# A two-layer hybrid encoder on one core: sums in their own banks, 192 keys, stepped pooling, and weight tiles prepared in quarters

## The reference

```
h = x @ w_in[l]                      # aq, ak, av, bq, bk, bv, cx
oa = local attention: 6 heads, chunks of 64 queries, each sees its own
     chunk of 64 keys and the one before, bias, softmax with a sink logit
ob = differential attention: 6 heads, two maps of 32 dims each,
     w = softmax(map 0) - lam * softmax(map 1), causal by chunks of 64
oc = pooling: means over windows of 2, 4, 8, 16 tokens less the input,
     a 64x64 matrix for each of 4 groups, times a scale
x = layer_norm(ALPHA * x + concat(oa, ob, oc) @ w_o[l])
u = conv3(x @ w_up[l]);  x = layer_norm(ALPHA * x + (silu(g) * u) @ w_down[l])
```

## Time and profile before

| what | value |
|---|---|
| median of 3 runs | 2726.92 us (2726.09 to 3502.72) |
| the profiled execution | 2722.3 us |
| its span | 2720.5 us |
| mean granted TensorE clock | 0.963 |
| instructions | 30437 |
| DMA | 249.03 MB, mean 92 GB/s |

### The profile page before, as it was taken

How to read it: one execution, slowest core, us unless ns; L and a number is a source line. 1 busy time by engine, 2 the same in 40 slices (tenths; PEclk the granted TensorE clock), 3 DMA queues, 4 the chain that set the end, 5 groups by cost and what they waited for, 6 DMA issues and landing times.

```text
span 2720.5 us, 30437 instructions
## 1 busy us (share of the span) xinstructions
PE 2491.2 (92%) x11608; PEld 2007.4 (74%) x11608; DVE 1503.7 (55%) x2845; ACT 831.3 (31%) x1709; POOL 1290.0 (47%) x724
## 2 busy tenths in 40 slices
PE   7987888999999999899998999988999989999996
PEld 5865666777777877777776877767777777788885
DVE  5256545566666385147666288056555555546436
ACT  1133314444442121035543122034444411222221
POOL 4532353434443655454444655543343445566662
PEclk7998999999999999999999999989999999999998
DMA  5633223332322323433322323432232122334331
GB/s 163 197 84 88 83 79 88 82 90 77 93 63 62 94 77 101 117 96 105 88 84 63 90 73 108 119 95 74 78 82 77 57 77 78 93 97 121 108 94 70
DMA packets 347264, 249.03 MB, mean 92 GB/s; under 512 B 37291, under 2 KB 306927, under 8 KB 347119
## 3 DMA queue, kind: packets, MB, share of 16 engines
q1 hardware_dynamic: 321792, 211.01, 26.2%
q10 hardware_dynamic: 25327, 36.07, 5.1%
HBM read 226.32 MB, written 20.71 MB: 91 GB/s over the span
## 4 chain that ended last, share of the span: by engine, by line
PE 65%; DVE 21%; ACT 5%; issue 4%; DMA 2%; POOL 1%; ACTq 1%; SPq 0%; DVEq 0%
PE psum L716 41%; PE psum L946 10%; PE psum L815 4%; PE psum L746 3%; PE psum L767 3%; DVE room L1209 3%; DVE room L1233 2%; DVE conv L1316 2%; PE psum L801 2%; ACT conv L1137 2%; DVE x_res L1520 2%; DVE conv L1338 2%; DMA w_raw<-in_w_in 1%; ACTq L981 1%; DVE x_res L1485 1%
## 5 line engine op out<-in xcount | busy, mean ns | idle before, releaser
L692 POOL CAST w_hi<-w_raw 128x1024 fp32r<-128x1024 f32 x360 | 405.2, 1125 | 1364.2 <-DMA w_raw<-in_w_up 699.7
L694 POOL TENSOR_TENSOR w_lo<-w_raw,w_hi 128x1024 fp32r<-128x1024 f32 x360 | 888.7, 2469 | 28.8
L716 PE MATMUL psum<-x_hi,w_hi 128*128 128x512 f32 x2048 | 848.5, 414 | 40.3 <-POOL w_lo L694 15.2
L716 PE MATMUL psum<-x_hi,w_lo 128*128 128x512 f32 x2048 | 814.4, 398 | 0.0
L716 PE MATMUL psum<-x_lo,w_hi 128*128 128x512 f32 x2048 | 813.2, 397 | 0.0
L716 PEld LDWEIGHTS psum<-x_hi,w_hi 128*128 128x128 f32 x2048 | 394.8, 193 | 139.1 <-issue 22.9
L946 PE MATMUL psum<-hid,w_hi 128*128 128x512 f32 x1408 | 451.2, 402 | 17.6 <-DVE x_res L1520 15.0
L716 PEld LDWEIGHTS psum<-x_hi,w_lo 128*128 128x128 f32 x2048 | 393.4, 192 | 87.8
L716 PEld LDWEIGHTS psum<-x_lo,w_hi 128*128 128x128 f32 x2048 | 395.8, 193 | 73.1 <-issue 1.7
L1316 DVE SCALAR_TENSOR_TENSOR conv<-psum,prm_all,conv 128x511 f32<-128x511 f32 x176 | 131.8, 749 | 490.1 <-ACT conv L1137 489.7
L946 PEld LDWEIGHTS psum<-hid,w_hi 128*128 128x128 f32 x1408 | 258.1, 191 | 79.1 <-DVE hid L1343 10.9
(11 more groups left out here) (126 smaller groups left out, 2339.0 us busy)
## 6 DMA issues: line engine op xcount, KB each, us to landing
w_raw<-in_w_up SPq DMA_DIRECT2D x176, 512.0 KB, 3.8
w_raw<-in_w_down SPq DMA_DIRECT2D x88, 512.0 KB, 3.6
w_raw<-in_w_in SPq DMA_DIRECT2D x36, 512.0 KB, 4.0
w_raw<-in_w_o SPq DMA_DIRECT2D x32, 512.0 KB, 4.1
qk_scratch<-stage_qk SPq DMA_DIRECT2D x48, 256.0 KB, 3.4
q_stack<-qk_scratch ACTq DMA_DIRECT2D x72, 128.0 KB, 2.9
k_stack<-qk_scratch ACTq DMA_DIRECT2D x36, 256.0 KB, 4.9
w_raw<-in_w_in SPq DMA_DIRECT2D x16, 384.0 KB, 3.4
```

The lines of the kernel that those rows point to most:

```text
L692: nc.gpsimd.tensor_copy(w_hi[:, slot, :], w_raw[:, slot, :]).then_inc(s["w_high"], 1)
L694: nc.gpsimd.tensor_tensor(w_lo[:, slot, :], w_raw[:, slot, :], w_hi[:, slot, :].bitcast(F32), ALU.subtract).then_inc(s["w_ready"], 1)
L716: mm = nc.tensor.matmul(o, w, v[:, k, :], start=(k == 0 and w is wh and v is x_hi[h]), stop=(k == KT - 1 and w is wl))
```

## The change

1. POOL cuts each tile in quarters of 256 columns: four casts without a wait between them, then four subtractions, each after its cast; the last one signals.
2. AV takes a dense bank of its own. `place_banks` gives each user of a dense bank (R, P and W of layer 0, V of layer 0, U, D, AV) the bank whose last user stands earliest in the list, and each bank has its own full and free semaphores. The waits for o_read are gone; the wait is for the bank.
3. Local heads leave out the 64 masked keys (`unseen`): scores, bias, exponential over 192 columns; the first of the two sums has 64 rows. The turning still takes both blocks whole.
4. Pooling is cut into events CW, two additions at a time, and `project` has a new order: c0, CW, bq0, CW, bk0, W0, c1, CW, bq1, CW, bk1, CW, bq2, W1, bk2, ak. `stages` is fitted to it; event PR now comes after two projected blocks instead of three.
5. V tiles of (0, 1) are no longer cut in parts and stand ahead of attention (0, 0), outside of the merge.
6. Shares: AV 0.6 to 0.9, AT 0.6 to 0.8, CW 1.0 each.

The core of the diff, without the many lines in which only a semaphore's name changes:

```diff
+    out = p("c0") + c((0, 0)) + p("bq0") + c((0, 1)) + p("bk0") + [("W", l, h, 0)] + p("c1") + c((1, 0))
+    out += p("bq1") + c((1, 1)) + p("bk1") + c((1, 2)) + p("bq2") + [("W", l, h, 1)] + p("bk2", "ak")
+    if (l, h) == (0, 1):
+        return values + out + p("aq0", "aq1", "aq2")
+    return out + values + [("AS", l, h)] + p("aq0", "aq1", "aq2")
...
-    return {"AV": 0.6, "AT": 0.6, "V": 0.5, "MR": 2.0, "LM": 2.0, "LE": 2.0, "LF": 1.5}.get(kind, 1.0)
+    return {"AV": 0.9, "AT": 0.8, "CW": 1.0, "V": 0.5, "MR": 2.0, "LM": 2.0, "LE": 2.0, "LF": 1.5}.get(kind, 1.0)
...
-    out = [("X", 0, i) for i in range(HT)] + first[:3] + [("PR",)] + first[3:4] + bias[:6] + first[4:5] + bias[6:]
-    out += [("N", 0)] + first[5:6] + [("N", 1)] + first[6:9] + [("N", 2)] + first[9:11] + [("N", 3)]
+    out = [("X", 0, i) for i in range(HT)] + first[:3] + [("PR",)] + first[3:5] + bias[:6] + first[5:7] + bias[6:]
+    out += [("N", 0)] + first[7:10] + [("N", 1)] + first[10:13] + [("N", 2)] + first[13:16] + [("N", 3)]
...
-    out += merge(left[:cut[0]], attend(0, 0))
+    out += left[:HT] + merge(left[HT:cut[0]], attend(0, 0))
...
+def unseen(h, u):
+
+    kind, head, t = unit_of(u)
+    return HD if kind == "a" and h * HT + t > 0 else 0
...
+def place_banks():
+
+    bank, read = {}, [-1] * 4
+    for e in EVENTS:
...
+        for key in keys:
...
+            n = min(range(4), key=lambda n: read[n])
+            assert read[n] < AT[e]
+            bank[key], read[n] = n, AT[last]
+    return bank
...
-                nc.gpsimd.tensor_copy(w_hi[:, slot, :], w_raw[:, slot, :]).then_inc(s["w_high"], 1)
-                pool.wait_ge(s["w_high"], n + 1)
-                nc.gpsimd.tensor_tensor(w_lo[:, slot, :], w_raw[:, slot, :], w_hi[:, slot, :].bitcast(F32),
-                                        ALU.subtract).then_inc(s["w_ready"], 1)
+                cuts = [slice(c, c + 256) for c in range(0, 1024, 256)]
+                for cut in cuts:
+                    nc.gpsimd.tensor_copy(w_hi[:, slot, cut], w_raw[:, slot, cut]).then_inc(s["w_high"], 1)
+                for q, cut in enumerate(cuts):
+                    pool.wait_ge(s["w_high"], 4 * n + q + 1)
+                    i = nc.gpsimd.tensor_tensor(w_lo[:, slot, cut], w_raw[:, slot, cut],
+                                                w_hi[:, slot, cut].bitcast(F32), ALU.subtract)
+                i.then_inc(s["w_ready"], 1)
...
-                for c in range(0, width, HALF):
+                for c in range(skip, width, HALF):
...
-                if u >= 1 and width_of(h, u)[1] > HALF:
-
-                    pe.wait_ge(s["o_read"], after(("AV", l, h, u - 1), "o_read"))
...
-                if u >= 1:
-                    pe.wait_ge(s["o_read"], after(("AV", l, h, u - 1), "o_read"))
+                take(e)
                 for b in range(width // P):
+                    seen = slice(unseen(h, u) if b == 0 else 0, P)
+                    mm = nc.tensor.matmul(ring_bank(e)[:, 0:HD], turned_w[h][seen, b * P:(b + 1) * P],
+                                          v_all[seen, lo + b, at:at + HD],
...
-                for dst in ((b1, b2) if c == 0 else (b1, b2, b1, b2)):
-                    at += w
-                    then(nc.vector.tensor_tensor(dst[:, at:], last[:, at:], last[:, at - w:HALF + PADC - w], ALU.add))
-                    last, w = dst, 2 * w
+                if step <= c:
+                    for last, dst, n in ((xs, b1, 0), (b1, b2, 1)) if step == 0 else ((b2, b1, 2), (b1, b2, 3)):
+                        w = 1 << n
+                        at = 2 * w - 1
+                        then(nc.vector.tensor_tensor(dst[:, at:], last[:, at:], last[:, at - w:HALF + PADC - w], ALU.add))
+                    return
```

More of the change, by code:

```diff
@@ L72, in project, with c @@
 def project(l, h):
[L73 to L77, removed]
     def p(*names):
[L80 to L86, removed]
+        out = []
+        for n in names:
+            if (l, h) == (0, 1):
+                out += [("Pp", l, h, n, part) for part in range(PARTS - 1)]
+            out.append(("P", l, h, n))
+        return out
+    values = [("V", l, h, i) for i in range(HT)]
+    def c(*steps):
+        return [("CW", l, h, *step) for step in steps]
+    out = p("c0") + c((0, 0)) + p("bq0") + c((0, 1)) + p("bk0") + [("W", l, h, 0)] + p("c1") + c((1, 0))
+    out += p("bq1") + c((1, 1)) + p("bk1") + c((1, 2)) + p("bq2") + [("W", l, h, 1)] + p("bk2", "ak")
+    if (l, h) == (0, 1):
+        return values + out + p("aq0", "aq1", "aq2")
+    return out + values + [("AS", l, h)] + p("aq0", "aq1", "aq2")
 def attend(l, h):
@@ L253, in signals @@
         if what[:2] == "aq":
-            if r == "d":
-                return {"d_full": 1, "d_free": 3 * (what == "aq2")}
+            if e[1] == 0:
+                out = {r + "_full": 1}
+                if what == "aq2":
+                    out |= {ring_of(("P", *e[1:3], f"aq{n}")) + "_free": 1 for n in range(PAIRS)}
+                return out
             return {"aq0": {}, "aq1": {"sb_full": 1},
@@ L264, in signals @@
         return out
+    if kind == "CW":
+        return {"pooled": 1} if e[3:] in ((0, 1), (1, 2)) else {}
     if kind == "V":
@@ L268, in signals @@
         if e[1] == 0:
-            return {"d_full": 4, "d_free": 4}
+            return {f"d{n}_{what}": 1 for n in range(4) for what in ("full", "free")}
         return {"sb_full": 1, "sb_free": 1, "tb_full": 1, "tb_free": 1}
@@ L340, with full, free @@
 assert len(AT) == len(EVENTS)
+def place_banks():
+    bank, read = {}, [-1] * 4
+    for e in EVENTS:
+        kind, keys = e[0], []
+        if kind in ("R", "D", "AV") or (kind in ("P", "W") and e[1] == 0 and e not in bank):
+            keys = [e]
+        elif kind == "Pp" and e[4] == 0:
+            keys = [("P",) + e[1:4]]
+        elif kind == "U" and e[5] == 0:
+            keys = [e[:5]]
+        elif kind == "V" and e[1] == 0 and e[3] == 0:
+            keys = [("V", *e[1:3], t) for t in range(HT)]
+        for key in keys:
+            last = key
+            if kind == "U":
+                last = key + (PARTS - 1,)
+            elif kind == "V":
+                last = ("V", *e[1:3], HT - 1)
+            elif key[0] == "P" and key[3][:2] == "aq":
+                last = ("P", *e[1:3], "aq2")
+            n = min(range(4), key=lambda n: read[n])
+            assert read[n] < AT[e]
+            bank[key], read[n] = n, AT[last]
+    return bank
+BANK = place_banks()
+def full(e):
+    return ring_of(e) + "_full"
+def free(e):
+    return ring_of(e) + "_free"
 def totals():
@@ L386, in ends @@
     if kind == "U":
-        return tile[:5] + (PARTS - 1,), "d_full"
+        last = tile[:5] + (PARTS - 1,)
+        return last, full(last)
     if kind == "D":
-        return tile[:4] + (tile[4] + 3,), "d_full"
+        last = tile[:4] + (tile[4] + 3,)
+        return last, full(last)
     if kind == "V":
@@ L739, in values @@
                         take(e, "tb")
-                for t in range(part * HT // parts, (part + 1) * HT // parts):
+                for t in range(HT):
                     cut = slice(t * P, (t + 1) * P)
```

181 lines of the change are left out of this document (91 added, 90 removed).

## The result

| | before | after |
|---|---|---|
| median of the runs | 2726.51 us (4 runs, 2724.18 to 3502.72) | 2655.45 us (4 runs, 2646.91 to 2665.05) |
| ratio, 95% interval | | 0.9743 [0.9698, 0.9788] |
| profiled execution | 2722.3 us, span 2720.5, clock 0.963 | 2659.14 us, span 2657.2, clock 0.971 |

A forecast was written before the change was run, and what follows sets the result against it. The prediction took PE, busy 92% of the span, plus its gaps and slow-clock spells as the bound. Its terms summed to -66 us, 2656 against the profiled execution; adjusted to the median it said 2660 us, range 2600 to 2745.

The forecast's parts named there:

- Ports: POOL's quartered tiles: fewer DVE collisions on shared SBUF ports, -40 us; added instructions making tiles ready later, +7 us.
- Rival C: POOL runs its four casts and four subtractions as one, so splitting doesn't free DVE: 2701 us, chance 0.12.
- Dense banks: AV sums in dense banks: waits for the last output's read go, half returning, -28 us; new bank waits +6.
- Rival A: Attention's waits only move: PE's return at the scores, banks give only -10 us; 2707 us, chance 0.15.
- 192 keys: Local heads' scores over 192 columns save PE, DVE and ACT work, the 64-row sum costing the same: -9 us.
- Steps and shares: Stepped pooling ends a 3.13 us start wait and frees DVE; new shares thin filler at mixing and norms: -6 us.
- V ahead: V of (0,1) ahead of the first attention takes 21.8 us of filler out of it: +12 us (0 to +22).
- Clock: With fewer PE gaps some of the time lost at the low granted clock comes back: -8 us (+5 to -25).
- Rival B: Gains compound in attention: PE's idle time halves and the clock comes back; 2630 us or 2600, chance 0.15.
- Rival D: POOL becomes the bound in the dense stretches between attentions, tiles slower than PE's pace: about 2770 us, chance 0.08.

The follow-up runs named there:

- after_alternate: The kernel after, but each POOL quarter's subtraction directly behind its cast with a wait between: 2643.8 us, ratio 0.9688 to the kernel before.
- before_v_first: The kernel before, only with the V tiles of half (0, 1) ahead of the first attention: 2751.17 us, ratio 1.0083 to the kernel before.

## Why the prediction was right, and where not

The sum held (-66 forecast, -63 between the profiled executions, -71 between the medians), but by errors of both signs, and that is partly luck. Taken out of after one at a time, the parts give: quarters -33, waits -43, steps up to -15, keys +16, shares 0; V +23 (in before). That adds up to -52; the other 19 us of the 71 aren't assigned to a part.

1. **Ports: -40 +7.** The mechanism is right and the term was too small: the quarters alone give -54, on top of the other edits -33. L1300's mean is 269 ns (announced: below 300), L1296's total 91.9 us (below 110), POOL's busy time 1626 us (1500 to 1650). The excess that I put at 200 us is 222. The step that failed is "DVE gets in between two POOL instructions, even back to back", and with it the announced longest waits near 0.7 us. It holds for 218 of 227. The row it rested on, the handover at 508 us, comes from a kernel in which POOL pauses after every cast, and so never has more than two instructions in a row; it couldn't show what a longer row does. Rival C, which I had as all or nothing, happens nine times, at a price of some 11 to 15 us. The -40 itself rested on 58 us for the part of 128 that is on the chain; by my own figures, 54 of 137.6, it is 50. The price of a quarter was close: 0.40 and 0.74 us measured, 0.36 and 0.70 forecast. From whole to quarters this is (4 x 0.400 - 1.042) / 3 = 0.19 us for each added cast and (4 x 0.737 - 2.397) / 3 = 0.18 us for each added subtraction, where I had 0.1.

The Trainium skill (SBUF — State Buffer, Who interferes with whom) says that the engine which issues first holds the shared ports for its whole instruction. That agrees with the trace of after_alternate, where the subtraction of 0.74 us that starts at 2401.92 takes 1.59, since DVE's L1562 (2401.54 to 2402.92) came first. That the one waiting may be passed over by 7 to 18 instructions of the other is what the nine show.

2. **Dense banks: -28 +6.** Mis-sized. Putting the waits back costs 43 us, three quarters of the 59 that they had held. I let half of it return at the scores, and only 3 us did (L819, 24.6 against 21.6), with 7 more at the sums' wait for ACT's copy (28.1 to 34.9), a row that I hadn't named. The new bank waits, +6, didn't come: L996's entry is 12.4 us where L946's was 15.0. Rival A is off by this too: the waits were worth 43 us, where it has 10.

3. **192 keys: -9.** Wrong in sign, as far as three pairs with overlapping intervals can tell. The score's part was right (8 us measured against 9.9), the failed step is "the 64-row sum costs the same". The two sums of a local unit take 925 ns instead of 590 behind a dense matmul, 25 us over all of them, and the whole edit loses 8 to 16 us.

4. **Steps and shares: -6.** The stepping gives up to 15 us, by a comparison whose intervals overlap; the shares nothing. The 3.13 us of issue at the start are gone, but what is late next there is a load, which I hadn't named: the event PR now comes before a parameter has landed. The chain of after at that place:

```profile
24.21 8.95 DMA area<-in_b_subln_g
```

PE stands still for 3.2 us, up to 33.2 us, against 3.1 before: one wait took the other's place.

5. **V ahead: +12.** It costs 23 in before. I bounded it by PE's work against latency, and left out that the clock in the attention may fall when the filler leaves it (0.93 to 0.82 in before_v_first): the upper bound of 22 was none. In the kernel with the pause, moving V behind the attention changed nothing that the medians show.

6. **Clock: -8.** 0.963 to 0.971 over the span as announced, but with a rise in the wide attentions (0.97 and 0.95 to 0.98) and a fall in the first (0.94 to 0.86). What this rise is worth was not measured by itself.

Rival B's way, gains that feed each other in the attentions, is near to what happened: PE's idle time in these three attentions went from 104 to 55 us. Against it stood the keys (8 to 16 us), V (23 us, measured in before) and the nine long waits (some 11 to 15 us). Rival D didn't happen: PE waits 19.8 us for POOL, 4.6 more than before.

## What to carry to other kernels

Where GpSimd and VectorE both stream from SBUF all the time, cut GpSimd's work into short instructions and leave a real wait between them; here short ones back to back let VectorE in after one or two pieces in 218 of 227 meetings and shut it out for 4.0 to 9.9 us in nine. A smaller matmul isn't a cheaper one until its start-to-start time, with that of its neighbours, is read from the trace, by shape. When work is moved out of a stretch that waits on a chain of other engines, ask what it does to the granted clock, not only to the gaps.

## What was unexpected of the hardware

- A DVE instruction with two SBUF inputs can be passed over by 7 to 18 POOL instructions in a row (up to 9.9 us). None of the eight kernels here in which POOL pauses for 0.08 us after each cast shows one; all six with quarters back to back do (9 to 13 each).
- Two float32 sums, of which the first has 64 rows take 925 ns behind a dense matmul, two of 128 rows 590. The first load of 64 rows behind others has 357 ns of idle time before it that no semaphore explains.
- The same 510 matmuls of the first attention run at a granted clock of 0.93 or 0.83 and take 126 or 139 us, with 22 us of idle time in both, depending on something that this case leaves open.
